# The SSD branch's x rows made token-major by DRAM regathers and a 32x32 transposition on VectorE, in place of TensorE transposes

## The reference

```python
h = rms_norm(x, norm_w) * (1 + scale) + shift
xbc, z_m, dt, u, v, z_g, gl_m, gl_g = split(h @ w_in)
xs, bm, cm = split(silu(dwconv5(xbc)))             # xs: 16 heads of 64 channels
y_m = rms_norm((ssd(xs, dt, a, bm, cm, h0) + d_skip * xs) * silu(z_m))
y_g = gelu(u) * spatial(layer_norm(gelu(v))) * silu(z_g)
merged = sigmoid(gl_m) * (y_m @ w_out_m) + sigmoid(gl_g) * (y_g @ w_out_g)
x = x + gate * (merged @ w_out)
```

## Time and profile before

| | before |
|---|---|
| median of 3 runs | 1440.16 us (1439.85 to 1440.32) |
| the profiled execution: span, first to last instruction | 1438.0 us |
| granted TensorE clock, mean | 0.998 |
| busy PE / DVE / ACT / POOL | 99% / 68% / 33% / 71% |
| HBM read, written | 169.79 MB, 18.15 MB |

### The profile page before, as it was taken

The page is one execution under the profiler, slowest core; times in us unless marked ns, Lnnn a source line. Parts: engine busy times, 40 slices in busy tenths (PEclk is TensorE's granted clock), DMA queues, the critical chain, the costliest instruction groups (busy, mean ns, idle before and its releaser), DMA issues.

```text
span 1438.0 us, 27064 instructions
## 1 busy us (share of the span) xinstructions
PE 1422.0 (99%) x10191; PEld 1382.6 (96%) x10191; DVE 983.8 (68%) x1454; ACT 474.4 (33%) x1086; POOL 1027.1 (71%) x1421
## 2 busy tenths in 40 slices
PE   8999999999999999999999999999999999999997
PEld 5999998999999999999999999989999999999997
DVE  5865566674777679889978676567566876868234
ACT  4332223313766423101243323241257661320122
POOL 1688875596655489998859897558765556979772
PEclk9999999999999999999999999999999999999999
DMA  9222333123566465444332242411346665453222
GB/s 359 60 64 75 130 108 121 56 70 110 150 189 192 144 262 197 144 164 145 113 133 74 79 128 87 137 60 59 103 127 182 170 189 187 159 188 120 74 74 89
DMA packets 113838, 189.54 MB, mean 132 GB/s; under 512 B 12736, under 2 KB 76352, under 8 KB 112320
## 3 DMA queue, kind: packets, MB, share of 16 engines
q1 hardware_dynamic: 42736, 138.34, 28.8%
q10 hardware_dynamic: 70992, 49.63, 11.7%
HBM read 169.79 MB, written 18.15 MB: 131 GB/s over the span
## 4 chain that ended last, share of the span: by engine, by line
PE 96%; DVE 2%; DMA 0%; ACT 0%; issue 0%; DVEq 0%; SPq 0%; ACTq 0%
PE acc L603 78%; PE acc L570 6%; PE X L843 2%; PE X L808 2%; PE X L570 1%; PE X L828 1%; PE X L875 1%; PE X L854 1%; PE X L762 1%; DVE cv L1631 1%; PE acc L721 0%; DVE ssq L1432 0%; DMA xr<-in_xT 0%; DVE h_pre L1484 0%; DVE xr L1949 0%; PE X L815 0%
## 5 line engine op out<-in xcount | busy, mean ns | idle before, releaser
L513 POOL CAST w_hi<-w_st 128x256 fp32r<-128x256 f32 x704 | 419.3, 609 | 388.7 <-issue 187.3
L517 POOL TENSOR_TENSOR w_lo<-w_st,w_hi 128x256 fp32r<-128x256 f32 x704 | 645.8, 927 | 0.0
L603 PE MATMUL acc<-h_hi,w_hi 128*128 128x320 f32 x1744 | 406.2, 314 | 0.8 <-ACT h_hi L1049 0.8
L603 PE MATMUL acc<-h_lo,w_hi 128*128 128x320 f32 x1744 | 397.8, 309 | 1.5 <-DVE h_lo L1478 1.5
L603 PE MATMUL acc<-h_hi,w_lo 128*128 128x320 f32 x1744 | 397.4, 309 | 0.0
L603 PEld LDWEIGHTS acc<-h_hi,w_hi 128*128 128x128 f32 x1744 | 288.6, 188 | 10.6 <-issue 7.5
L603 PEld LDWEIGHTS acc<-h_lo,w_hi 128*128 128x128 f32 x1744 | 291.5, 188 | 2.2 <-DVE h_lo L1478 2.0
L603 PEld LDWEIGHTS acc<-h_hi,w_lo 128*128 128x128 f32 x1744 | 291.5, 188 | 0.0
L1631 DVE SCALAR_TENSOR_TENSOR cv<-raw,convw_sb,cv 128x642 f32<-128x642 f32 x128 | 134.9, 1054 | 4.5
L1391 DVE SCALAR_TENSOR_TENSOR ada_acc<-ada_st,sc,ada_acc 128x512 f32<-128x512 f32 x112 | 107.1, 995 | 1.8
L1145 ACT ACTIVATE cvt<-cv 128x642 f32<-128x642 f32 x32 | 23.8, 743 | 158.1 <-DVE cv L1631 158.1
(11 more groups left out here) (257 smaller groups left out, 2468.4 us busy)
## 6 DMA issues: line engine op xcount, KB each, us to landing
w_st<-in_wts SPq DMA_DIRECT2D x176, 512.0 KB, 3.6
cum_bc<-cum_dram ACTq DMA_DIRECT2D x80, 256.0 KB, 5.0
ada_st<-in_wada SPq DMA_DIRECT2D x33, 512.0 KB, 4.4
ex_bc<-ex_dram ACTq DMA_DIRECT2D x64, 128.0 KB, 3.2
ada_pre<-in_wada SPq DMA_DIRECT2D x15, 512.0 KB, 10.0
mga_dram<-c_buf SPq DMA_DIRECT2D x16, 320.0 KB, 6.0
xf<-xf_dram SPq DMA_DIRECT2D x4, 1280.0 KB, 7.2
mga<-mga_dram SPq DMA_DIRECT2D x2, 2560.0 KB, 9.9
```

The lines of the kernel that those rows point to most:

```text
L513: nc.gpsimd.tensor_copy(quarter(w_hi, slot, q), quarter(w_st, slot, q)).then_inc(s_pool, 1)
L517: nc.gpsimd.tensor_tensor(quarter(w_lo, slot, q), quarter(w_st, slot, q), f(quarter(w_hi, slot, q)), ALU.subtract).then_inc(w_split, 1)
L603: last = mm(a[:, hf, 0:n1], w[:, s, cols], x[:, k, hf * HALF:hf * HALF + n1], start=(k == 0 and n == 0), stop=(k == KC - 1 and n == 2))
```

## The change

- The PE transposes of xs (80, five for each of eight tiles in two layers), their two ACT copies each (32) and the waits that went with them (`tp_ready`, `tp_out`, and one on `v_made` for the two blocks in tile 24) are gone.
- `xf_dram` is now laid out by chunk: (5 chunks, 128 channels, 8 tiles, 128 tokens). ACT stores each `xo` as before with two DMAs, but in pieces of 512 bytes, and at another place in its list: ahead of the next conv's tanh (tiles 13, 14, 18 to 21), or in a v tile (15, 22) ahead of what stands there.
- SP gathers each tile back in four DMAs, one for each group of 32 tokens, into 32 partitions each (640 pieces of 128 bytes a DMA), into `xs0` or `xs1`, behind the weights of tiles 17, 18, 19 and 22 to 26 (`XG_AT`). It waits for the store, and for the turn that frees the buffer.
- DVE turns `xs` into `x_tok` with one 32x32-block transposition of 128x640 (`x_turn`): three after conv 10, one after conv 13, one after conv 14, three after conv 15 (`XT_AT`), each ahead of the a units there.
- The reload of `xf` becomes eight DMAs of 640 pieces of 512 bytes, where it was two with 10,240 bytes a partition.

```diff
-X_AT = [(p + 2, 4) for p in CONV_AT[8:14]] + [(24, 3), (24, 6)]
+XS_AT = {p + 1: j for j, p in enumerate(CONV_AT[8:])}
+XG_AT = {p + 5: j for j, p in enumerate(CONV_AT[8:])}
+XT_AT = {10: (0, 1, 2), 13: (3,), 14: (4,), 15: (5, 6, 7)}
-    xf_dram = nc.dram_tensor("xf_dram", (P, KC, TOK), F32, kind="Internal").ap()
+    xf_dram = nc.dram_tensor("xf_dram", (NCH, P, KC, P), F32, kind="Internal").ap()
+    xs = [place(f"xs{i}", [P, NCH, 4, 32], r_c + i * TOK * 4) for i in range(2)]
+        def x_gather(L, j):                                   # SP, after weight(t)
+            if j >= 2:
+                sp.wait_ge(xt_done, 8 * L + j - 1)
+            else:
+                sp.wait_ge(tmT_ready, L + 1)
+            sp.wait_ge(xf_stored[j % 2], 32 * (KC // 2 * L + j // 2 + 1))
+            src = xf_dram[:, :, j, :].rearrange("c (b f) (q t) -> q f (c b) t", f=32, t=32)
+            for q in range(4):
+                sp.dma_start(xs[j % 2][32 * q:32 * (q + 1), :, :, :].rearrange("p c b t -> p (c b) t"), src[q])\
+                    .then_inc(xs_in[j % 2], 16)
-                for i, k in enumerate((slice(0, KC // 2), slice(KC // 2, KC))):
-                    sp.dma_start(xf[:, k, :], xf_dram[:, k, :]).then_inc(xf_in[i], 16)
+                for k in range(KC):
+                    sp.dma_start(xf[:, k, :].rearrange("p (c n) -> p c n", n=P),
+                                 xf_dram[:, :, k, :].rearrange("c p n -> p c n")).then_inc(xf_in[2 * k // KC], 16)
-        def transposes(src, n):                               # PE
-            if n > 1:
-                pe.wait_ge(tp_out, n - 1)
-            for c in range(NCH):
-                last = nc.tensor.transpose(xcols((X[0], X[1]), c), src(c), ident[:, :])
-            last.then_inc(tp_ready, 1)
-                tp_copy(x_tok[:, :, P * j:P * (j + 1)], 8 * L + j + 1)
-                act.dma_start(xf_dram[:, j, 0:CTX], xo[:, j % 2, 0:CTX]).then_inc(xf_stored[j % 2], 16)
-                act.dma_start(xf_dram[:, j, CTX:TOK], xo[:, j % 2, LAT0:LAT0 + LAT]).then_inc(xf_stored[j % 2], 16)
+            def x_store(j):                                   # ACT
+                act.wait_ge(conv_done, NCONV * L + 9 + j)
+                act.dma_start(xf_dram[0, :, j, :], xo[:, j % 2, 0:CTX]).then_inc(xf_stored[j % 2], 16)
+                act.dma_start(xf_dram[1:NCH, :, j, :].rearrange("c p n -> p c n"),
+                              xo[:, j % 2, LAT0:LAT0 + LAT].rearrange("p (c n) -> p c n", n=P)).then_inc(xf_stored[j % 2], 16)
             def conv_tanh(i):
...
+                if CONV_AT[i] in XS_AT:
+                    x_store(XS_AT[CONV_AT[i]])
                 A(cvt[:, 0:CW], cv[:, i % 2, 0:CW], ACT.Tanh).then_inc(cvt_ready, 1)
...
+                    if p in XS_AT:                            # v tiles
+                        x_store(XS_AT[p])
                     copies(p + 1)
...
+            def x_turn(j):                                    # DVE, after conv i, ahead of the a units
+                if L > 0 and j == 0:
+                    dve.wait_ge(x_stored, 16)
+                dve.wait_ge(xs_in[j % 2], 64 * (KC // 2 * L + j // 2 + 1))
+                nc.vector.transpose(x_tok[:, :, P * j:P * (j + 1)], xs[j % 2][:, :, :, :].rearrange("p c b t -> p (c b t)"))\
+                    .then_inc(xt_done, 1)
```

More of the change, by code:

```diff
@@ L114 @@
 B_AT = [(T_G - 2, 4), (T_G - 1, 8)] + [(p, k + 1) for p, k in B_AT[2:]]
-STANDS = sorted([(at, "a", n) for n, at in enumerate(A_AT)] + [(at, "x", n) for n, at in enumerate(X_AT)]
+STANDS = sorted([(at, "a", n) for n, at in enumerate(A_AT)]
                 + [(PBB_AT, "pbb", 0)]
@@ L336, in build @@
     pads_ready, cv_ready, cvt_ready, conv_done = sem("pads_ready"), sem("cv_ready"), sem("cvt_ready"), sem("conv_done")
-    tp_ready, tp_out, ln_ready = sem("tp_ready"), sem("tp_out"), sem("ln_ready")
+    xs_in, xt_done, ln_ready = [sem("xs_in0"), sem("xs_in1")], sem("xt_done"), sem("ln_ready")
     bt_mm, bt_ready, xw_ready, s_mm, s_out = sem("bt_mm"), sem("bt_ready"), sem("xw_ready"), sem("s_mm"), sem("s_out")
@@ L453, in _ @@
             weight(t, t % 2)
+            if p in XG_AT:
+                x_gather(L, XG_AT[p])
             j = (p - T_G - 5) // 2
@@ L554, in v_tile @@
                     pe.wait_ge(v_made, KC // 2 * (t // NT) + j)
-                if j == 3:
-                    pe.wait_ge(tp_out, 8 * (t // NT) + 6)
                 if ready is not None:
@@ L859, in pbb_products @@
             pe.wait_ge(wsp_in, 48 * (L + 1))
-            pe.wait_ge(tp_out, 8 * (L + 1))
             pe.wait_ge(v_made, KC // 2 * (L + 1))
@@ L896, in _ @@
             h = (h_hi, h_lo)
[L898 to L902, removed]
             def stand(what, n):
-                return lambda: {"a": lambda: a_burst(L, n), "x": lambda: x_transposes(n),
+                return lambda: {"a": lambda: a_burst(L, n),
                                 "pbb": lambda: pbb_products(L),
@@ L1014, in final_weight @@
             A(xr[:, k, rows], xr[:, k, rows], ACT.Copy, scale=finalw_sb[:, k:k + 1]).then_inc(fw_ready, 1)
[L1016 to L1020, removed]
         act.wait_ge(c_in, 16)
@@ L1148, in copies @@
                 for k, what, n in stands(p):
-                    if what == "x":
-                        x_copy(n)
-                    elif what == "a":
+                    if what == "a":
                         a_copies(n)
@@ L1246, in _ @@
                             evacuated(act, t - 2)
+                        else:
+                            act.wait_ge(xt_done, 8 * (L + 1))
                         A(halves(c_buf[0]), acc_of(t)[:, :, 0:HALF], ACT.Tanh, scale=0.5).then_inc(zt_ready, 1)
@@ L1611, in a_unit @@
                 n = NU * L + a
-                dve.wait_ge(tp_out, 8 * L + 2 * g + 2)
+                dve.wait_ge(xt_done, 8 * L + 2 * g + 2)
                 if a >= 2:
@@ L1644, in _ @@
                     if i >= 10:
-                        dve.wait_ge(tp_ready, 8 * L + i - 9)
                         dve.wait_ge(xf_stored[i % 2], 32 * (KC // 2 * L + (i - 10) // 2 + 1))
@@ L1663, in _ @@
                     state_weights()
+                for j in XT_AT.get(i, ()):
+                    x_turn(j)
                 for a in {10: (0, 1), 11: (2,), 12: (3,), 13: (4,), 14: (5, 6), 15: (7, 8)}.get(i, ()):
@@ L1791, in _ @@
                     dve.wait_ge(zt_ready, 16 * L + j + 1)
+                    if n == 1:
+                        dve.wait_ge(xt_done, 8 * (L + 1))
                     free(t, STT(out=halves(c_buf[1]), in0=halves(c_buf[0]), scalar=1.0,
@@ L1830, in add_skip @@
                 y = xf[:, j, :].rearrange("p (c n) -> p c n", n=P)
-                dve.wait_ge(xf_in[2 * j // KC], 16 * (L + 1))
+                dve.wait_ge(xf_in[2 * j // KC], 16 * KC // 2 * (L + 1))
                 return own.mark(STT(out=y, in0=y, scalar=dcol[:, j:j + 1], in1=x_tok[:, :, P * j:P * (j + 1)],
```

3 lines of the change are left out of this document (removed).

## The result

The changed kernel takes 1445.54 us (median of 13 runs, 1443.14 to 1452.67), the kernel before 1440.18 us (13 runs, 1439.85 to 1442.48): a ratio of 1.0042, 95% interval 1.0031 to 1.0054. It is slower, by 5.4 us where 2.0 were forecast, and its runs spread over 9.5 us, which the kernel before doesn't do. The profiled execution (1447.54 us) is one of the longer ones, with a span of 1445.8 us against 1438.0.

What follows compares the result with a forecast made beforehand. PE, busy 99% of the span, was taken to bound the kernel. In span 1438.0 - 8.8 + 6.0 + 0.3 + 4.5 = 1440.0, so 1442.2 us against the median of 1440.16; range 1436.5 to 1450.

Steps and rivals of the forecast that it cites:

- rival A: The forecast itself: waits at burst (24,2) and tile 58 both paid; 1442.2 us, own range 1439.5 to 1445; chance 0.50.
- rival E: Gathers come late, DVE's units make PE wait at (25,5) or in tiles 19 to 24: 1445.2 us; chance 0.09.
- part 1: PE's list: removing the transposes saves 0.55 us a block, 16 blocks, 8.8 us.
- ring at (24,2): PE, DVE and ACT chain from burst (23,2) through conv 15's tanh, product and bt to (24,2); 3.0 us longer a layer.
- part 2: ACT's list, (23,2) to (24,2): stores ahead of tanh and bt delay PE's burst, +6.0 us for two layers.
- part 3: DVE's list, convs 12 to 14: with stores and turns DVE just keeps up, 0.8 us left; +0.3 us.
- part 4: SP's gathers: even with dear prices the last is in time for unit 7 at burst (25,5); 0 us.
- part 5: Reload of xf: 512-byte pieces delay tile 58's weight, so PE waits there; +4.5 us for both layers.
- Rival B: ACT's list: works ahead of its DMA issues, ring costs under 1 us; 1436.2 us; chance 0.10.
- d: At the reload of xf: how much later tile 58's weight comes, 2.7 us; bounds 0 and 11.
- Rival C: Reload of xf: 512-byte pieces take no longer, by the line-rate rule; 1437.7 us; chance 0.10.
- Rival D: Reload of xf slow, pieces 4 KB apart in DRAM: 1458.8 us at 56 ns a piece, 1450.8 at 40; chance 0.17.

Runs made afterwards that it cites:

- b2: Kernel before with four of five PE transposes of each x block left out (result not the reference's, for time alone): 1433.07 us, ratio 0.9948.
- a5: Changed kernel with stores behind tanh and bt, units 7 and 8 ahead of turns 6 and 7, weight of tile 58 ahead of the reload: 1434.16 us.
- a4: Changed kernel with SP issuing the weight of tile 58 ahead of the reload of xf: 1442.95 us, ratio 1.0017 to before.
- a1: Changed kernel with ACT's stores of xo moved behind the tanh and the copies of bt and states: 1445.41 us, ratio 1.0037 to before.
- b1: Kernel before, PE's transposes kept, with the change's layout by chunk, 512-byte stores and reload in eight DMAs: 1443.91 us, ratio 1.0031.
- b3: b1 with the reload in five DMAs, one a chunk, in place of eight: 1449.42 us, ratio 1.0065 to before.
- c1: a5 with the store of conv 14's xo also behind the copy of bt, and DVE's last turn behind unit 9: 1431.08 us, ratio 0.9935 to before.
- a2: Changed kernel with DVE's units 7 and 8 ahead of turns 6 and 7: 1444.72 us, ratio 1.0028 to before.
- a7: a5 with the conv tiles' stores back ahead of the tanh: 1435.27 us, ratio 0.9966 to before.
- a6: a5 with the v tiles' stores back ahead of bt: 1438.53 us, ratio 0.9984 to before.

## Why the prediction was right in sign and range, and 3.3 us short

1445.5 lies in the range of 1436.5 to 1450, but 0.5 above rival A's own (1439.5 to 1445), which was the forecast proper. It is next to rival E's 1445.2, though E's reason made up only a small part of it.

Terms, in us for both layers, forecast and as the profiled execution shows them:

| term | forecast | measured |
|---|---|---|
| blocks off PE (part 1) | -8.8 | -8.8 taken; -9.2 by b2 |
| ring at (24,2), idle (part 2) | +6.0 | 3.54 + 3.56 - 2 x 0.23 = +6.6 |
| clock behind it | 0 | 4.00 x 0.41 + 3.60 x 0.44 = +3.2; by the starts of (24,2) and (25,2), 9.69 + 9.72 less 2 x 8.12 (a5) = +3.2 |
| DVE's list (part 3) | +0.3 | 0 (2.83 us idle left) |
| last gather, (25,5) (part 4) | 0 | 0.90 + 0.35 = +1.25 |
| reload, idle (part 5) | +4.5 | 0.26 + 2.65 = +2.9 |
| clock behind it | 0 | 4.00 x 0.36 = +1.4, and a little after |

They sum to +6.6 of the 7.8 us between the two spans; 1.2 us I can't place. In the median run the reload is 2.6 us in all (changed kernel less a4).

- **Part 1** was right. b2 measured it by itself.
- **Part 2** was right in mechanism, place and length. "3.36 us after the tanh starts" was 3.63, the idle time 3.54. Rival B fell: ACT does wait behind its issues. The step that failed is the price of the wait, in parts 2 and 5 alike: the sum had each us of waiting at one us. Behind 3.5 us of idleness the matmuls ran for most of 4 us at half speed, 1.6 us a layer. The kernel before has no idle time of this length in its tiles, so none of its rows shows the price. The Trainium skill's page "TensorE: Matmul & The Clock Gate", HAM oscillation, warns of idle gaps after which the engine starts at the low level again, and the forecast had not weighed it; the trace agrees, with 0.59 and 0.56 behind 3.54 and 3.56 us.
- **Part 3**: right that DVE keeps up, with more to spare than the 0.8 us I left it.
- **Part 4** failed as "in time with dear prices all along". Four issues took 3.88 us where 2.4 was put, the landing 5.8 where 3.6 was: the last gather shares the DMA engines with the loads of wsp and the bias that ACT issues there (from 228.2 to 234.0 us SP's queue took 57.3% of the 16 engines and ACT's 36.9%). That these loads are what made it late is argued: no run moved them. SP's timeline:

```profile
224.34 3.88 SPq L442 DMA_DIRECT2D xs<-xf_dram  x4
228.27 1.00 SPq L420 DMA_DIRECT2D w_st<-in_wts  x1
```

  It cost only 1.25 us because the ring made PE late as well; a1 shows its full price, 3.85 and 3.47 us of idleness and a slow clock. And the forecast didn't see that units 7 and 8 need x of tiles 2 and 3 alone, so that they were behind that gather by the list's order only. That is rival E's place, hidden behind A's.
- **Part 5** was right in mechanism and near in price: 27.5 ns a piece forecast, 29.6 measured; d = 2.7 forecast, 1.5 and 3.5 in the two layers of the profiled execution, 2.4 and 2.2 in b1. The slack ahead of tile 58 was put too small, at 0.6 and 0.3 us where 1.3 and 0.8 were there, in the main because the split was taken at the 2.05 us that it has beside DVE's work. Rival C, the Trainium skill's rule of line rate from 512 bytes ("DMA: Bandwidth & Descriptors", Specifications), fell: 302 GB/s against 405. Rival D's reason fell by b3; 29.6 ns is already at the 29 from which D was to decide, and the larger slack is what kept the waits at 0.26 and 2.65 us. That this term would vary by several us from run to run wasn't foreseen, nor the slow clock behind its wait.

So of the miss of 3.3 us 2.9 are explained: +3.2 for the clock, +1.3 for the gather and +0.6 for the ring, less 0.3 for DVE's list and 1.9 for a reload dearer on paper (4.5) than in the median run (2.6, its clock included). The errors have both signs, and it is luck that the miss isn't larger: with the reload at its forecast 4.5 us the time would have been 1445.5 + 1.9 = 1447.4, 5.2 above the forecast.

What stays open: what made the last gather late, why the reload varies between runs (SP's eight issues took 6.46 us in layer 0 and 8.10 in layer 1 of one execution), and whether SP's issue or the transfer sets its end, since both grow with the number of pieces.

## What to carry to other kernels

Work taken off the bounding engine is worth its time only if the lists of the other engines can follow. Ahead of a removal, go through every list at the place where the bounding engine already waits a little, and put DMA issues behind what it waits for: here four issues in front of a tanh and a copy cost 3.3 us of waiting and 1.6 of slow clock a layer, more than the 4.4 us that the blocks gave, and moved back (c1) they cost nothing. After a wait is removed look for the next one behind it in the same chain (a1 was worth nothing without a2, both together 9.5 us). And a large transfer that nobody waits for yet should stand behind the smaller one that the bounding engine needs next.

## What the runs showed of the hardware

- **An idle TensorE can cost more than its idle time.** Waits of 1.10, 1.26 and 1.60 us (at (24,2) in a7, at tile 58 in a2 and a1) left the granted clock at 1.00; behind waits of 2.50 (a6), 2.65 and 3.54 (changed kernel) it was 0.69, 0.64 and 0.59 in the next 3 to 4 us. But the length of the wait alone doesn't decide. In b3 it fell behind 3.14 us of waiting in layer 0 and not behind 3.34 us in layer 1; windows of PE behind these two:

```profile
517.30:521.30 4.00, 4.00 (x19) 0.66 0.02 6
1220.00:1224.00 4.00, 4.00 (x27) 1.00 0.02 8
```

  A fall cost 1.5 to 1.6 us in both layers of the changed kernel and of a6. It cost 2.5 us in layer 1 of a2, where the same stretch from (24,2) to (25,2) took 10.65 us: the clock already read 0.50 before PE went on, and stayed there longer.

- **Reads in 512-byte pieces run at three quarters of the rate of 2,560-byte ones** (302 and 389 GB/s), whichever way they lie in DRAM.
- **ACT starts a DMA issue while an ACTIVATE ahead of it in the list still runs, but in these rows no ACTIVATE passes an issue.** In c1 two issues start at 217.43 and 217.79, before two copies (217.89 and 218.16) that stand ahead of them. In a5 (tanh and issue start together, and the copy behind the issues waits):

```profile
219.16 0.74 ACT L1139 ACTIVATE cvt<-cv 128x642 f32<-128x642 f32 x1 [11.96 <-DVE cv L1637]
219.17 0.33 ACTq L1130 DMA_DIRECT2D xf_dram<-xo  x1
219.53 0.45 ACTq L1131 DMA_DIRECT2D xf_dram<-xo  x1
220.09 0.38 ACT L1117 ACTIVATE states<-X 128x256 f32<-128x256 f32 x1 [0.18 <-issue]
```
